# Score blocks without zero padding, and normalisation factors applied to products, in a two-layer hybrid decoder kernel

## The reference

```
x = x + Mixer(RMSNorm(x))
x = x + CrossAttn(RMSNorm(x), RMSNorm(mem))   # 4 heads of 256, 256 memory tokens
x = x + W2 relu(W1 RMSNorm(x))^2              # hidden 4096
```

```
o = q_t . S_chunk            # from the state at the chunk's start
  + sum_s scores[t, s] v_s   # within the chunk
S_next = decay * S + k^T v
```

## Time and profile before

| | |
|---|---|
| median of 3 runs | 2268.08 us (2265.14 to 2268.51) |
| the profiled execution's own time | 2266.12 us |
| its span | 2264.3 us |
| PE busy | 2101.5 us, 93% of the span |
| mean granted TensorE clock | 0.964 of full speed |
| DVE, ACT, POOL busy | 1023.3, 894.6 and 903.8 us |

### The profile page before, as it was taken

How to read it: one execution, slowest core, us unless ns; L and a number is a source line. 1 busy time by engine, 2 the same in 40 slices (tenths; PEclk the granted TensorE clock), 3 DMA queues, 4 the chain that set the end, 5 groups by cost and what they waited for, 6 DMA issues and landing times.

```text
span 2264.3 us, 34446 instructions
## 1 busy us (share of the span) xinstructions
PE 2101.5 (93%) x13340; PEld 1720.5 (76%) x13340; DVE 1023.3 (45%) x1521; ACT 894.6 (40%) x1520; POOL 903.8 (40%) x684
## 2 busy tenths in 40 slices
PE   3898989989999899999978898999999998999997
PEld 2777767777886688888857777787688867888886
DVE  4497764863314331112155867478353144212113
ACT  5453442424444343323254243443245344423322
POOL 1352333243652345445334252334256523445451
PEclk7999999999999999999989999999999999999998
DMA  4322222123331233333233222222234312333331
GB/s 148 78 66 53 75 66 70 39 85 112 121 118 55 75 95 97 98 98 98 71 84 74 64 68 66 65 72 85 71 98 132 115 43 79 97 96 96 98 98 61
DMA packets 205098, 191.32 MB, mean 84 GB/s; under 512 B 30242, under 2 KB 202620, under 8 KB 204540
## 3 DMA queue, kind: packets, MB, share of 16 engines
q1 hardware_dynamic: 204924, 189.01, 28.7%
HBM read 184.77 MB, written 3.15 MB: 83 GB/s over the span
## 4 chain that ended last, share of the span: by engine, by line
PE 75%; DVE 16%; ACT 5%; issue 2%; DMA 1%; SPq 1%; POOL 0%; DVEq 0%; ACTq 0%; another core or an unknown queue 0%
PE gemm L539 68%; PE mix L539 7%; DVE work L1456 6%; DVE work L1465 2%; DVE work L1542 1%; DVE gate_t L1465 1%; DVE h_lo L1465 1%; DMA small<-in_s_log_step_dram 1%; ACT w_hi L1023 1%; DVE merged L1456 0%; DMA w_raw<-in_w_in_dram 0%; POOL w_lo L530 0%; ACT L1109 0%; DVE merged L1465 0%; DVE s_small L1456 0%
## 5 line engine op out<-in xcount | busy, mean ns | idle before, releaser
L530 POOL TENSOR_TENSOR w_lo<-w_raw,w_hi 128x512 fp32r<-128x512 f32 x680 | 903.5, 1356 | 1323.2 <-ACT w_hi L1023 1323.2
L539 PE MATMUL gemm<-h_hi,w_hi 128*128 128x512 f32 (+1 forms) x1584 | 634.9, 401 | 35.0 <-DVE h_lo L1465 18.0
L539 PE MATMUL gemm<-h_lo,w_hi 128*128 128x512 f32 (+1 forms) x1584 | 624.6, 394 | 0.0
L539 PE MATMUL gemm<-h_hi,w_lo 128*128 128x512 f32 (+1 forms) x1584 | 623.4, 394 | 0.0
L539 PE MATMUL gemm<-work_split,w_hi 128*128 128x512 f32 (+1 forms) x1792 | 528.0, 379 | 0.0
L1023 ACT ACTIVATE w_hi<-w_raw 128x512 fp32r<-128x512 f32 x680 | 385.1, 619 | 290.3 <-DMA w_raw<-in_mlp_w_dram 186.5
L539 PEld LDWEIGHTS gemm<-h_hi,w_hi 128*128 128x128 f32 (+1 forms) x1584 | 301.6, 190 | 115.9 <-DVE h_lo L1465 28.6
L539 PEld LDWEIGHTS gemm<-work_split,w_hi 128*128 128x128 f32 x1792 | 330.7, 190 | 65.0 <-issue 4.0
L539 PEld LDWEIGHTS gemm<-h_hi,w_lo 128*128 128x128 f32 (+1 forms) x1584 | 301.4, 190 | 65.1
L539 PEld LDWEIGHTS gemm<-h_lo,w_hi 128*128 128x128 f32 (+1 forms) x1584 | 301.9, 191 | 64.1 <-issue 2.4
L539 PE MATMUL gemm<-work_split,w_lo 128*128 128x512 f32 (+1 forms) x896 | 337.8, 377 | 0.0
(11 more groups left out here) (265 smaller groups left out, 1689.4 us busy)
## 6 DMA issues: line engine op xcount, KB each, us to landing
w_raw<-in_mlp_w_dram SPq DMA_DIRECT2D x256, 256.0 KB, 2.7
w_raw<-in_w_in_dram SPq DMA_DIRECT2D x224, 256.0 KB, 2.8
w_raw<-in_xattn_w_kv_dram SPq DMA_DIRECT2D x64, 256.0 KB, 2.8
w_raw<-in_w_branch_dram SPq DMA_DIRECT2D x32, 256.0 KB, 2.8
w_raw<-in_w_out_dram SPq DMA_DIRECT2D x32, 256.0 KB, 2.7
w_raw<-in_xattn_w_q_dram SPq DMA_DIRECT2D x32, 256.0 KB, 2.8
w_raw<-in_xattn_w_o_dram SPq DMA_DIRECT2D x32, 256.0 KB, 2.8
work<-in_x_dram SPq DMA_DIRECT2D x4, 512.0 KB, 5.3
```

What stands on the lines that cost most here:

```text
L530: pool.tensor_tensor(lo, raw, hi.bitcast(F32), ALU.subtract).then_inc(split_ready, 1)
L539: return pe.matmul(o, w, a, start=start, stop=stop, skip_group_check=True)
```

## The change

The mixers: `outputs` takes the scores as they lie, as 64x64 blocks, with products of 64 rows, and puts even and odd chunks of a head pair in two banks instead of one, the part within chunks first for both pairs, then the part from the states. The block-diagonal copy and its memsets are gone for hg and gl (the mLSTM keeps its own), and so are the memsets of all states; a state is kept in the rows of its own head, and an update takes all heads of a tile in one operation. `head_out` collects each head pair from two banks, with 8 operations of 128x256 for 4 of 128x512. The mLSTM's outputs stay in their four banks, but its products with the states have 64 rows instead of 128.

The norms of cross-attention and MLP: ACT makes h_hi at once from X with the gain alone as its scale, while the squares are being taken; DVE makes h_lo from X and h_hi (`norm_low`). The token's factor is applied later. In cross-attention it scales the scores in the softmax's exponential and its bias (RC and RN); it is made per token by `norm_tokens`, 4 products with one column each, after `kv4`. In the MLP `norm(2)` stands after `up0_0`, and DVE takes relu and multiplies by the factor in one operation that reads PSUM; ACT squares and rounds. The attention's result is written to tiles of its own (OThi, OTlo), no longer over h.

```diff
+            def norm_tokens():
+                pe.wait_ge(sq_used, 7)
+                for t in range(TT):
+                    i = mm(M[3][:, t:t + 1], NS[:, t * P:(t + 1) * P], mean_w[:, 0:1])
+                i.then_inc(ms_done, 1)
...
             def outputs(m):
-                pe.wait_ge(m.bd_ready, 1)
                 pe.wait_ge(m.s_ready, 2)
                 for j in range(2):
-                    heads = [(h, slice(64 * (h % 2), 64 * (h % 2) + 64)) for h in (2 * j, 2 * j + 1)]
                     for t in range(TT):
-                        for h, rows in heads:
-                            mm(M[j][rows, t * P:(t + 1) * P], m.V[:, t, HD * h:HD * h + HD], m.attbd[:, m.slot(h), t, :], stop=False)
-                        for c in (2 * t, 2 * t + 1):
-                            for h, rows in heads if c else ():
-                                jt = h // m.per
-                                i = mm(M[j][rows, c * CH:(c + 1) * CH], m.S[:, jt, c - 1, HD * (h % m.per):HD * (h % m.per) + HD],
-                                       m.Q[:, jt * SEQ + c * CH:jt * SEQ + (c + 1) * CH], start=False, stop=True)
+                        for a in range(2):
+                            part = slice(64 * a, 64 * a + 64)
+                            for h in (2 * j, 2 * j + 1):
+                                rows = slice(64 * (h % 2), 64 * (h % 2) + 64)
+                                at_ = m.slot(h) * 256 + t * CH
+                                i = mm(M[2 * a + j][rows, t * CH:(t + 1) * CH], m.V[part, t, HD * h:HD * h + HD], m.att[part, at_:at_ + CH], start=t == 0, stop=False)
+                    i.then_inc(m.within, 1)
+                for j in range(2):
+                    pe.wait_ge(m.within, j + 1)
+                    for c in range(1, NCH):
+                        for h in (2 * j, 2 * j + 1):
+                            ...
+                            i = mm(M[2 * (c % 2) + j][rows, at_:at_ + CH], m.S[r0:r0 + m.dk, jt, c - 1, :],
+                                   m.Q[r0:r0 + m.dk, jt * SEQ + c * CH:jt * SEQ + (c + 1) * CH], start=False, stop=True)
                     i.then_inc(m.o_done, 1)
...
-                gemm("kv0", *mmin, n=MEM, ready=at["mm_ready"])
-                norm(1)
-                for c in range(1, 4):
-                    gemm(f"kv{c}", *mmin, n=MEM)
+                for c in range(4):
+                    gemm(f"kv{c}", *mmin, n=MEM, ready=at["mm_ready"] if c == 0 else None)
...
                     gemm(f"kv{4 + c}", *mmin, kind="tm", n=MEM)
+                    if c == 0:
+                        norm_tokens()
...
-                norm(2)
-
-                done = 0
                 for q in (0, 1):
                     for c in range(4):
                         gemm(f"up{q}_{c}", *H, ready=h_ready if (q, c) == (0, 0) else None, ready_at=16)
+                        if (q, c) == (0, 0):
+                            norm(2)
...
             def head_out(m):
                 for j in range(2):
                     act.wait_ge(m.o_done, j + 1)
-                    do(act.activation(m.O[:, j, :], M[j][:, :], ACT.Copy, scale=m.oscale))
-                    do(act.activation(m.SQ[:, j, :], M[j][:, :], ACT.Square, scale=m.oscale), head_sq)
+                    for a in range(2):
+                        chunks = lambda ap: ap[:, j, :].rearrange("p (t a c) -> p t a c", a=2, c=CH)[:, :, a, :]
+                        bank = M[2 * a + j][:, 0:256].rearrange("p (t c) -> p t c", t=TT)
+                        do(act.activation(chunks(m.O), bank, ACT.Copy, scale=m.oscale))
+                        do(act.activation(chunks(m.SQ), bank, ACT.Square, scale=m.oscale), head_sq if a else None)
...
-            def squares(n):
+            def squares(n, gain=None):
                 for k in range(KC):
                     feed_past((f"out{k // 2}", f"o{k // 2}", f"down3_{k // 2}")[n - 1])
                     act.wait_ge(x_ready, (0, 0, 8, 40)[n] + k + 1)
+                    if gain:
+                        do(act.activation(Hhi[:, k, :], X[:, k, :], ACT.Copy, scale=col(gain, k)), hi_ready)
...
-                squares(2)
+                squares(2, "norm_mlp")
                 factors(2)
-                norm_hi(2)
...
-                            do(act.activation(UPX[:, 0, :], bank[:, :], ACT.Relu), up_a)
-                            act.nop().then_inc(free, 1)
-                            act.wait_ge(up_v, n + 1)
-                            do(act.activation(MHID[q % 2][0][:, 2 * c + b, :], UPX[:, 0, :], ACT.Copy), uphi)
+                            do(act.activation(UPX[1], UPX[0], ACT.Square), up_a)
+                            do(act.activation(MHID[q % 2][0][:, 2 * c + b, :], UPX[1], ACT.Copy), uphi)
...
+            def norm_low(n, gain, k0, k1):
+                for k in range(k0, k1):
+                    dve.wait_ge(hi_ready, 8 * n + k + 1)
+                    stt(Hlo[:, k, :], X[:, k, :], col(gain, k), Hhi[:, k, :].bitcast(F32), ALU.mult, ALU.subtract, h_ready)
...
-                do(dve.memset(m.attbd[0:64, :, :, 64:128], 0.0))
-                do(dve.memset(m.attbd[64:128, :, :, 0:64], 0.0))
-                av = m.att.rearrange("p (h t c) -> p h t c", h=4, t=TT)
-                for a in range(2):
-                    rows = slice(64 * a, 64 * a + 64)
-                    do(dve.tensor_copy(m.attbd[rows, :, :, 64 * a:64 * a + 64], av[rows]), m.bd_ready if a else None)
-                do(dve.memset(m.S.rearrange("p j c v -> p (j c v)"), 0.0))
...
+                            dve.wait_ge(gemm_done[s], 2 * used + b + 1)
+                            if n[0]:
+                                dve.wait_ge(up_a, n[0])
+                            stt(UPX[0], G[s][b][:, :], 0.0, R(32)[:, 0, :], ALU.max, ALU.mult, up_v)
+                            dve.nop().then_inc(gemm_free[s], 1)
```

More of the change, by code:

```diff
@@ L1323, in kv_copy @@
                         act.nop().then_inc(free, 1)
-                squares(1)
+                squares(1, "norm_xattn")
                 act.wait_ge(at["mm_ready"], 8)
-                kv_copy(0)
-                factors(1)
-                for c in range(1, 4):
+                for c in range(4):
                     kv_copy(c)
-                norm_hi(1)
                 def exponentials(h):
@@ L1376, in _ @@
                     for c in range(4):
-                        for b, bank, free in banks(f"up{q}_{c}"):
+                        feed_past(f"up{q}_{c}")
+                        for b in range(2):
+                            act.wait_ge(up_v, n + 1)
                             if n:
                                 act.wait_ge(uplo, n)
-                            else:
-                                act.wait_ge(h_ready, 24)
                             if q >= 2 and (c, b) == (0, 0):
```

117 lines of the change are left out of this document (61 added, 56 removed).

## The result

The changed kernel takes 2245.59 us (median of 4 runs, 2241.35 to 2248.03) against 2267.35 of the kernel before, measured beside it: ratio 0.9906, 95% interval 0.9887 to 0.9924, so 1% faster, 21 us. The forecast was 2241 us in a range of 2234 to 2252.

A forecast was written before the change was run, and what follows sets the result against it. PE was taken as the bound, busy 2101.5 of 2264.3 us. From the profiled 2266.1 us, -24.5 (norms), -1.6 (outputs) and nothing for `up` gave 2240.0, from the median 2242; 2241 was said, range 2234 to 2252.

The forecast's parts named there:

- Part 1: Cross-attention and MLP norms: four gaps worth 28.5 us go, less new mean and wait costs in two layers; -24.5 us.
- the mean in the stream: MLP norm's mean product, formerly hidden in the gap, now costs PE 0.9 us a layer.
- the new wait for POOL in `up0_1`: PE waits once for the second weight unit of `up0_1`, since ACT stands waiting for the mean; 1.1 us a layer.
- Part 2: Outputs of the three mixers: mLSTM -0.5, hg +0.8, gl -1.1 us a layer; -1.6 us over two layers.
- mLSTM -0.5: mLSTM's outputs: 112 instructions with states go from 29 to 24 ns each, saving 0.5 us a layer on PE.
- ACT's copies: Behind hg's and gl's outputs, eight smaller copies replace four and finish later; 0.8 us a layer at each place.
- gl's wait: PE's 1.86 us wait for DVE's states before gl's outputs goes entirely; less ACT's 0.8, saves 1.1 us a layer.
- Part 3: `up` tiles: same operations in another order, bank free after DVE's first; costs nothing, with 5 us cover per block.
- B: Rival: the clock falls behind `norm(2)` or after `kv4`, seven slow steps costing 1.7 us a place; 2248 us, chance 0.10.
- C: Rival: blocks without common rows and columns run side by side, small products costing 12 to 15 ns; 2237 us, chance 0.08.
- D: Rival: 64-row products with changing rows take 55 ns each, lengthening all mixers' outputs; 2261 us, chance 0.05.
- E: Rival: `up` tiles become the bound through DVE, 1.1 us lost in each of 32 blocks; 2276 us, chance 0.03.

The follow-up runs named there:

- e1: The kernel before with only the norm and MLP edits, mixers as before; 2244.8 us, ratio 0.9902.
- e2: The kernel before with only the mixers' edits, both norms as before; 2266.56 us, ratio 0.9991.
- e10: The whole change with idle DVE copies and zeroings in gl, enough to bring back PE's wait before gl's outputs; 2244.81 us, ratio 0.9895.
- e4: The whole change with gl's state products taking four array quarters in turn and mLSTM's within-chunk products all before its state products; 2242.06 us, ratio 0.9892.
- e5: The whole change measured again, nothing altered; 2245.74 us, ratio 0.9906.
- e6: The whole change with the second norm's mean product moved back directly behind `o3`, ahead of `up0_0`; 2255.44 us, ratio 0.9951.
- e8: The whole change with about 12 us of idle DVE work in gl, meant to restore PE's wait there but making none; 2246.52 us, ratio 0.9918.

## Why the prediction was right, and where it was not

**Part 1, the norms, -24.5 us: right.** The four stretches gave 23.8 and 24.1 us, e1 as a whole 24.5 by its median and 22 by its ratio. Its terms held, though the MLP's gain was 8.4 and 7.0 us in the two layers where 7.5 and 9.0 were put: in cross-attention 4.66 and 3.71 us came where 4.72 and 3.31 were put; the mean in the stream costs 1.79 - 0.91 = 0.88 us (forecast 0.9); the new wait for POOL in `up0_1` makes its product 0.86 us late and the five behind it 0.12 (forecast 1.1), and came where it was said. Counted from the last product of `o3`, the mean came after 11.11 us and Ln after 12.17, where 11.2 and 12.3 had been put; POOL's unit took 1.33 us (793.37 to 794.70) and not 1.49, hence the shorter wait.

**Part 2, the outputs, -1.6 us: not refuted as a sum, wrong in its terms.** e2 measured -2 +-2. The terms were: mLSTM -0.5, measured +0.44 a layer. The step that failed is "for the mLSTM the 112 instructions with states go from 29 to 24 ns": they stay at 29 ns, since the two blocks of a pair alternate as before, and three switches between 128 and 64 rows of 0.15 us come on top. hg's outputs were put at 2.9 us and took 2.79; ACT's copies cost less than the 0.8 us put for them: POOL started 0.43 us later than before (at 205.56, 10.16 us after the outputs' start, against 203.16, 9.73 us). In layer 1 nothing of that reached PE, by luck, since POOL's first unit had taken 1.84 us before; in layer 2 PE resumed 0.53 us later (11.58 against 11.05), and e1 has both cases as well, so the cost is 0.3 us a layer on average. Behind gl's outputs the same copies cost 0.33 us (the mean starts 3.85 us after them, before 3.52), not 0.8. gl's wait went as forecast, but 1.86 us were booked for it where e10 and the 18 stretches show 0.6: the wait was cover for a fall of the clock that came in two of three cases. The term was sized from one execution in which no fall came. Put right, the terms are 2 x (0.44 + 0.3 + 0.33 - 0.6) = +0.9 us, not -1.6, while e2 as a whole has -2 (-4.3 to +0.2). What makes up the difference is not shown, so that the sum came out near is luck as far as its terms go.

**Part 3, up: right.** PE's timeline has no wait between 794.70 and the next layer's norm in layer 1.

**The rivals.** B's price of slower products behind the mean came at neither place. C's mechanism is true where four different quarters of the array take turns: there instructions start 15 ns apart. It did not hold for what C priced: mLSTM's two blocks share no rows and no columns, and start 29 ns apart on average as full rows did. Only the products within chunks of hg and gl got four quarters, not the ones with states. "TensorE: Matmul & The Clock Gate" of the Trainium skill, section "Part 3: Packing small matmuls — row/col tiling", has the overlap as a rule; the trace agrees, once four quarters are in turn, and the scores, from which I argued against it, use only two at a time. Their 24 ns were also misread: the 1.56 us hold the last instruction's own duration, and from start to start the 64 instructions are 21 ns apart, which is under the floor of 25 ns that the prediction found in agreement. The floor of about 25 ns from start to start that the Trainium skill states (the same page, section "Wait — 56ns, not 53.3ns?") does not hold for small f32 instructions in different quarters: the windows of e4 have 56 instructions in less than 1.1 us. D and E did not come.

**The time.** 2241 was forecast, 2245.6 and 2245.7 were measured, and the range held both. About 26 us less were forecast and 21 to 22 measured. Of the missing 4 to 5 us, part 1's stretches hold 0.5; part 2's terms put right would hold 2.5, but e2 as a whole does not show them; the rest is within the intervals and not attributed. The clock alone moves more than that: the same TensorE program took 882.8 to 892.8 us in the mixers. What decides where the clock falls is open. The mixers' program of the change gave 888 us on average (the change, e2, e5, e6 and e8), that of before 886 (before and e1); with 10 us between executions this shows no difference. Two of the signs named for "right" did not come: the wait for POOL after hg's outputs is 2.31 us and not 3 to 3.5, and the mean granted clock is 0.963 (0.964 in e5) and not above 0.964.

## What to carry to other kernels

A factor that is one number for a token can be applied behind the product; the larger gain is then often that the reduction's own product can move behind the next block, so that the engine in order never waits for it. Where one engine does both the copies of a stage and the preparation of the next weights, look for a wait with such a preparation behind it: three early splits, with mLSTM's order of products (0.3 us a layer), gave 1% here, as much as the whole change. A short wait that follows a place where the clock may fall is worth less than its length, and a single trace can't price it.

## What the runs showed of the chip

Small f32 instructions of 64 columns start 15 ns apart when four different quarters of the array take turns (e4), and 29 ns apart in the products with states when two do (the change); the scores, which change their two quarters from head to head, come to 21 ns. A switch between products of 128 and of 64 rows costs 0.15 us (e4 against the change). And one TensorE program differed by 10 us of 885 in its mixers' stages between three executions (the change, e5 and e8), 1.1%, with the mean granted clock between 0.963 and 0.965 each time: the mean clock of a page is too coarse to see it, a window over the stretch is not.
